# A decoder step on one core: levels 32 and 64 of a triangular inverse as products of 32x32 and 64x64 tiles, and the modulation in column halves

## What is computed

```python
for layer in range(DEPTH):                                  # DEPTH = 2, D = 1024
    mod = (silu(c) @ w_ada[layer] + b_ada[layer])           # c: 9 rows (prompt + 8 sequences), w_ada: 1024 x 6144
    shift1, scale1, gate1, shift2, scale2, gate2 = split(mod, 6)
    h = rms_norm(x, g_norm1[layer]) * (1 + scale1) + shift1
    proj = h @ w_in[layer]
    o_a = gdn_mixer(...)                                    # gated delta rule, 4 heads x 128, below
    o_b = conformer_conv(...)                               # causal depthwise convolution of width 31
    x = x + gate1 * (concat([o_a, o_b]) @ w_out[layer])
    h = rms_norm(x, g_norm2[layer]) * (1 + scale2) + shift2
    f = swiglu(h, ...) if layer == 0 else moe_swiglu(h, ...)  # dense, then top 2 of 8 experts
    x = x + gate2 * f
# inside the gated delta rule, for each head and block of tokens:
a_mat = where(strict, (k * beta) @ k.T * decay, 0.0)
t_inv = triangular_solve(eye + a_mat, eye)                  # inverse of a unit lower triangular matrix
u, w = t_inv @ (v * beta), t_inv @ (k * beta * exp(gc))
```

## Time and profile before

| | |
|---|---|
| median of 3 runs | 1647.95 us (1646.57 to 1649.50) |
| the profiled execution: time | 1647.72 us |
| its span in the trace | 1645.9 us |
| busy in the span | PE 98%, PEld 55%, DVE 47%, ACT 23%, POOL 8% |
| the chain that ended last | PE 90%, DVE 6%, ACT 2%, DMA 1% |
| mean granted clock of PE | 0.979 |

### The profile page before, as it was taken

How to read it: one execution, slowest core, us unless ns; L and a number is a source line. 1 busy time by engine, 2 the same in 40 slices (tenths; PEclk the granted TensorE clock), 3 DMA queues, 4 the chain that set the end, 5 groups by cost and what they waited for, 6 DMA issues and landing times.

```text
span 1645.9 us, 31324 instructions
## 1 busy us (share of the span) xinstructions
PE 1612.4 (98%) x12975; PEld 902.8 (55%) x12975; DVE 773.0 (47%) x1852; ACT 378.3 (23%) x617; POOL 123.5 (8%) x162
## 2 busy tenths in 40 slices
PE   6999999999999999999999999999999999999997
PEld 3878977999998879763333333333333333333333
DVE  2799656454438995462323333334234243243254
ACT  3346524443334454220001010010010100100102
POOL 0122205000012121030000000000000000000100
PEclk9999999999999998978999999999999999999999
DMA  9877029983647760165999999999999999999998
GB/s 383 347 304 257 27 84 370 410 317 128 241 147 301 290 270 1 58 245 194 397 404 407 420 421 410 420 411 420 418 401 420 420 410 420 401 421 420 405 421 372
DMA packets 82375, 535.35 MB, mean 325 GB/s; under 512 B 9184, under 2 KB 9312, under 8 KB 23488
## 3 DMA queue, kind: packets, MB, share of 16 engines
q1 hardware_dynamic: 70592, 487.46, 73.7%
q0 software_dynamic: 10080, 40.47, 6.3%
q10 hardware_dynamic: 1568, 5.51, 0.9%
HBM read 516.24 MB, written 36.04 MB: 336 GB/s over the span
## 4 chain that ended last, share of the span: by engine, by line
PE 90%; DVE 6%; ACT 2%; DMA 1%; issue 1%; SPq 0%; DVEq 0%
PE ps L2448 44%; PE ps L2457 6%; PE ps L1933 6%; PE ps L1934 5%; PE ps L1935 5%; PE ps L2122 4%; PE ps L2293 4%; PE ps L2474 3%; DVE yc L1337 2%; PE ps L1944 1%; PE ps L2030 1%; PE ps L2045 1%; PE ps L2043 1%; PE ps L1984 1%; PE ps L2063 1%; PE ps L2430 1%
## 5 line engine op out<-in xcount | busy, mean ns | idle before, releaser
L2474 PE MATMUL ps<-raw,hT 128*32 128x512 f32 x996 | 432.8, 592 | 0.0
L2474 PE MATMUL ps<-extra,hT 128*32 128x512 f32 x972 | 421.9, 592 | 0.0
L2448 PE MATMUL ps<-extra,ht 128*32 128x512 f32 x2736 | 403.4, 595 | 0.7 <-DVE ht L1843 0.7
L2448 PE MATMUL ps<-raw,ht 128*32 128x512 f32 x2640 | 387.8, 592 | 0.0
L1858 DVE TENSOR_TENSOR ae<-ps,sge 96x512 f32<-96x512 f32 x56 | 38.4, 686 | 514.9 <-PE ps L2448 514.9
L2448 PEld LDWEIGHTS ps<-extra,ht 128*32 128x32 f32 x2736 | 109.2, 110 | 270.4 <-issue 270.3
L2448 PEld LDWEIGHTS ps<-raw,ht 128*32 128x32 f32 x2640 | 104.9, 110 | 256.9 <-issue 256.1
L1819 DVE STREAM_TRANSPOSE hT<-ae 32x128 f32<-32x128 f32 x672 | 202.9, 302 | 17.8
L1210 ACT ACTIVATE sge<-ps 96x512 f32<-96x512 f32 x56 | 33.2, 592 | 705.8 <-PE ps L2448 705.6
L1933 PE MATMUL ps<-h_hi,whi 128*128 128x288 f32 x560 | 168.3, 300 | 0.2 <-DVE h_lo L1321 0.2
L1934 PE MATMUL ps<-h_lo,whi 128*128 128x288 f32 x560 | 166.2, 297 | 0.0
(11 more groups left out here) (367 smaller groups left out, 1804.7 us busy)
## 6 DMA issues: line engine op xcount, KB each, us to landing
raw<-units SPq DMA_DIRECT2D x279, 1024.0 KB, 12.2
extra<-units SPq DMA_DIRECT2D x174, 1024.0 KB, 13.9
slots_in<-const_in POOLq DMA_DIRECT2D x18, 512.0 KB, 30.6
slots_out<-const_in POOLq DMA_DIRECT2D x18, 512.0 KB, 31.6
raw<-units SPq DMA_DIRECT2D x16, 512.0 KB, 7.1
sst<-gdn_in POOLq DMA_DIRECT2D x8, 512.0 KB, 7.3
gdns_out<-sst POOLq DMA_DIRECT2D x8, 512.0 KB, 4.0
qst_out<-qpad POOLq DMA_DIRECT2D x2, 1890.0 KB, 10.7
```

The lines of the kernel that those rows point to most:

```text
L2448: last = mm(ps[rows(t), (G_BANK if kind == "g" else U_BANK) + n % 2, :], ht[n // FC % 2][:, a], weights((kind, n, k // 4), k % 4), start=( ...
L2474: last = mm(ps[GROUPS * GT:P, DOWN_BANK[t][half], :], hidden(n, t, k), weights(("d", n, half), k), start=(c == 0 and first), stop=(n in st ...
```

## The change

Two edits. At levels 32 and 64, `level_pm` and `level_q` multiply only the tiles that are not zero, and `inverse_level` subtracts only these; `tiles_at(s)` gives the ranges of rows and columns of the upper and the lower half of each diagonal square. Levels 2 to 16 and the sample block stay as they are, and so do `level_mask` and `copy_pm` at all levels. In the modulation, a partial sum now takes two of the eight parts more into one accumulation, and the four quarters of the partitions hold two column halves times two partial sums; so the tile is 128 x 256, the copy half as wide, and `ada_columns` has two products with 18 moving columns for four with 9.

```diff
--- before.py
+++ after.py
@@ -245,8 +245,9 @@
 FAR = 30000.0
 LOG_EXP = "natural_log_exp_and_others"
 LEVELS = [2, 4, 8, 16, 32, 64]
+TILED = 32
 CCOL, NCONST = columns(
-    [("ones", P), ("comb", NC_), ("eps6", 1), ("eps5", 1), ("epsq", 1), ("one", 1), ("ident", P), ("tri", P), ("after", P), ("m1l", P), ("m1t", P)]
+    [("ones", P), ("comb", 2 * NC_), ("eps6", 1), ("eps5", 1), ("epsq", 1), ("one", 1), ("ident", P), ("tri", P), ("after", P), ("m1l", P), ("m1t", P)]
     + [(f"mt{s}", P) for s in LEVELS] + [("outA", P), ("outQ", P), ("outAS", TS), ("outQS", TS)]
     + [("pick", 2 * 8), ("before", P), ("iota", P), ("triS", P), ("afterS", P), ("seqp", NB),
        ("ipart", 1), ("valid", 1),
@@ -284,7 +285,7 @@
     put("outQS", np.where(same & (i <= j), FAR, -FAR)[:TS, :TS])
     put("seqp", np.arange(P)[:, None] % TS // TD == np.arange(NB)[None, :])
     put("pick", np.concatenate([np.eye(P // 4)[:, P // 4 - 2 * 8:]] * 4))
-    put("comb", np.concatenate([np.eye(P // 4, NC_)] * 4) * (i % (P // 4) < NC_))
+    put("comb", np.kron(np.kron(np.eye(2), np.ones((2, 1))), np.eye(P // 4, NC_)))
     put("eps6", np.full((P, 1), 1e-6))
     put("eps5", np.full((P, 1), 1e-5))
     put("epsq", np.full((P, 1), P * 1e-6))
@@ -294,6 +295,11 @@
     put("rank", np.broadcast_to(NE - np.tile(np.arange(NE), 3)[None, :], (P, 3 * NE)))
     put("eye8", np.eye(NE))
     return c
+
+
+def tiles_at(s):
+
+    return [(slice(2 * s * j, 2 * s * j + s), slice(2 * s * j + s, 2 * s * (j + 1))) for j in range(P // (2 * s))]
 
 
 class Steps:
@@ -842,7 +848,7 @@
             def row_copy(l, m, place, bank):
                 n = ADA_AT[LANDS["ada", l, 2 * m + 1]]
                 act.wait_ge(ada_used, n + 1)
-                act.activation(modrow[place][n // 2 % len(modrow[place])][:, :], ps[:, bank, :], ACT.Copy).then_inc(row_ready, 1)
+                act.activation(modrow[place][n // 2 % len(modrow[place])][:, 0:2 * P], ps[:, bank, 0:2 * P], ACT.Copy).then_inc(row_ready, 1)
 
             def rsqrt(out, in_, scale, eps, done):
 
@@ -1493,6 +1499,14 @@
                 half = lambda t, i: t.rearrange("p (g c) -> p g c", c=2 * s)[:, :, i * s:(i + 1) * s]
                 L, LT = blk[b]["L"][0:n, 0:H * n], blk[b]["LT"][0:n, 0:H * n]
                 bank, c = Q_AT[blk_i]
+                if s >= TILED:
+                    L3, LT3, Q = heads(blk[b]["L"], n, n), heads(blk[b]["LT"], n, n), bank_heads(Q_AT[blk_i], n, n)
+                    for up, low in tiles_at(s):
+                        if not final:
+                            dve.tensor_tensor(L3[low, :, up], L3[low, :, up], Q[low, :, up], ALU.subtract)
+                        last = dve.tensor_tensor(LT3[up, :, low], LT3[up, :, low], Q[up, :, low], ALU.subtract)
+                    last.then_inc(l_ready, 1)
+                    return
                 if not final:
                     dve.tensor_tensor(half(L, 0), half(L, 0), half(ps[0:n, bank, c:c + H * n], 0), ALU.subtract)
                 dve.tensor_tensor(half(LT, 1), half(LT, 1), half(ps[0:n, bank, c:c + H * n], 1), ALU.subtract).then_inc(l_ready, 1)
@@ -1940,18 +1954,22 @@
                 for half in halves:
                     u = LANDS["ada", l, 2 * m + half]
                     pe.wait_ge(raw_in[u % NRAW], 16 * (u // NRAW + 1))
-                    for k in range(4):
-                        last = mm(ps[32 * k:32 * k + 32, bank, :], cst3[:, 4 * half + k], raw[u % NRAW][:, k * 512:(k + 1) * 512],
-                                  start=(half == 0), stop=(half == 1))
+                    for k in range(0, 4, 2):
+                        for q in range(4):
+                            a, p = divmod(q, 2)
+                            last = mm(ps[32 * q:32 * q + 32, bank, 0:2 * P], cst3[:, 4 * half + k + p],
+                                      raw[u % NRAW][:, (k + p) * 512 + 2 * a * P:(k + p) * 512 + 2 * (a + 1) * P],
+                                      start=(half == 0 and k == 0), stop=(half == 1 and k == 2))
                     last.then_inc(ada_used, 1)
 
             def ada_columns(l, m, place, bank=7):
 
                 n = ADA_AT[LANDS["ada", l, 2 * m + 1]] // 2
                 pe.wait_ge(row_ready, n + 1)
-                for q in range(4):
-                    c = (4 * m + q) * NC_
-                    last = mm(ps[:, bank, c:c + NC_], modrow[place][n % len(modrow[place])][:, q * P:(q + 1) * P], cc("comb"), start=True, stop=True)
+                cols = ps[:, bank, 4 * m * NC_:4 * (m + 1) * NC_].rearrange("p (a i c) -> p a i c", a=2, i=2)
+                for i in range(2):
+                    last = mm(cols[:, :, i], modrow[place][n % len(modrow[place])][:, i * P:(i + 1) * P],
+                              cc("comb").rearrange("p (a c) -> p a c", a=2), start=True, stop=True)
                 last.then_inc(modT_ready, 1)
 
             def ada_run(pairs, banks, place):
@@ -2020,15 +2038,19 @@
                     last = pe.transpose(bank_heads(AT_AT[blk_i], n, n)[:, h], heads(blk[b]["da"], n, n)[:, h], cc("ident", n, n))
                 last.then_inc(at_done, 1)
 
-            def level_pm(l, b, blk_i, n, q):
+            def level_pm(l, b, blk_i, n, q, s):
                 pe.wait_ge(mt_ready, 13 * l + q + 1)
                 if q in (0, 1, 12):
                     pe.wait_ge(low_ready, 3 * l + blk_i + 1)
                 else:
                     pe.wait_ge(l_ready, 13 * l + q - 1)
+                MT, L, PM = heads(blk[b]["MT"], n, n), heads(blk[b]["L"], n, n), bank_heads(PM_AT[blk_i], n, n)
                 for h in range(H):
-                    last = mm(bank_heads(PM_AT[blk_i], n, n)[:, h], heads(blk[b]["MT"], n, n)[:, h], heads(blk[b]["L"], n, n)[:, h],
-                              start=True, stop=True)
+                    if s < TILED:
+                        last = mm(PM[:, h], MT[:, h], L[:, h], start=True, stop=True)
+                        continue
+                    for up, low in tiles_at(s):
+                        last = mm(PM[low, h, up], MT[up, h, low], L[up, h, up], start=True, stop=True)
                 last.then_inc(pm_done, 1)
 
             def level_q(l, b, blk_i, n, q, s, final):
@@ -2038,6 +2060,15 @@
                     pe.wait_ge(linit_ready, 3 * l + blk_i + 1)
                     pe.wait_ge(qk_ready, 3 * l + blk_i + 1)
                 LT, PM = heads(blk[b]["LT"], n, n), heads(blk[b]["PM"], n, n)
+                if s >= TILED:
+                    Q = bank_heads(Q_AT[blk_i], n, n)
+                    for h in range(H):
+                        for up, low in tiles_at(s):
+                            if not final:
+                                mm(Q[low, h, up], LT[low, h, low], PM[low, h, up], start=True, stop=True)
+                            last = mm(Q[up, h, low], PM[low, h, up], LT[low, h, low], start=True, stop=True)
+                    last.then_inc(q_done, 1)
+                    return
                 if not final:
                     for h in range(H):
                         mm(half(bank_heads(Q_AT[blk_i], n, n)[:, h], 0), LT[:, h], half(PM[:, h], 0), start=True, stop=True)
@@ -2135,7 +2166,7 @@
                 cols = [slice(0, P), slice(P, 2 * P), slice(TP, T)]
                 for i in range(len(LEVELS)):
                     for b in range(2):
-                        level_pm(l, b, b, P, 2 * i + b)
+                        level_pm(l, b, b, P, 2 * i + b, LEVELS[i])
                     for b in range(2):
                         level_q(l, b, b, P, 2 * i + b, LEVELS[i], i == len(LEVELS) - 1)
 
@@ -2182,7 +2213,7 @@
                 outputs(l, 0, P)
                 state_rows(l, 0, 7)
                 conf_part(l, 0)
-                level_pm(l, 2, 2, TS, 12)
+                level_pm(l, 2, 2, TS, 12, 2)
                 pe.wait_ge(nw_ready, l + 1)
                 pe.wait_ge(s_ready, 2 * l + 1)
                 new_values(l, 1, P, 4)
```

## The result

The changed kernel takes 1650.68 us, the median of 20 runs (1645.05 to 1655.96), beside 1645.91 for 20 runs of the kernel before (1642.54 to 1651.17). The ratio is 1.0024, with a 95% interval of 1.0013 to 1.0035: 4.0 us slower, and clear of no change. The forecast was 1646.9 us against a median of 1647.95 for before, thus 1 us faster.

A forecast was written before the change was run, and what follows sets the result against it. TensorE was taken to bound the kernel, nine tenths of the span. Level 32 -3.2, norm -0.6, router -0.6, clock +1.4 and +2.2 made -0.8 us from 1647.72: forecast 1646.9 us, range 1642.5 to 1651.5.

The forecast's parts named there:

- the sum's clock term for the blocks: State products (L2063) in both layers' blocks: clock falls earlier, costing 1.1 us a layer, 2.2 in all, bounds 0 to 5.2.
- Level 64: Inverse, level 64: TensorE's work halves but is covered by 2.64 us of VectorE's other work, so counted as nothing.
- Where the clock is low now it can't fall twice: Layer 1's L2063, already part low: argument against the rival in which the clock decides; no size of its own.
- Level 32: Inverse, level 32: 32x32 products at 34 ns, subtractions 0.2 us apart; last correction 1.6 us earlier a layer, 3.2 for two.
- Layer 0's projection: Eight modulation pairs hidden behind VectorE; TensorE waits 2.9 us before the fourth sum of squares, low clock charged 1.4 us.
- Layer 1's projection: Four modulation pairs there, behind VectorE or ScalarE: no gain, and no clock charge.
- Modulation elsewhere: Pairs at layer 1's first norm save 0.6 us and those ahead of the router 0.6; row copy about 370 ns.
- the dense stage's part: One modulation pair in the dense stage: may give 0.4 us, left out of the sum.
- The clock decides: Rival: slack TensorE brings low clock after layer 0's wait and over all L2063; +4.1 us, 1651.8; chance 0.15.

The follow-up runs named there:

- e3: Kernel before with only level 64 of the inverse in tiles, level 32 and modulation as before: 1651.93 us, ratio 1.0040 to the kernel before.
- e4: Kernel before with levels 32 and 64 in tiles and unused TensorE products behind both levels' corrections, modulation as before: 1646.14 us, ratio 0.9997.
- e13: Kernel before with level 64 in tiles, two and four unused products there, and state products at 64 moving columns: 1638.66 us, ratio 0.9963.
- e15: Whole change plus unused products at both levels and layer 0's third sum of squares made four times, thin state products: 1643.35 us, ratio 0.9982 to before.
- e16: Kernel before with level 32 in tiles and unused products there, state products at 8 moving columns, modulation as before: 1646.23 us, ratio 1.0002.
- e14: Kernel before with level 32 tiles and unused products, 64-column state products, modulation in column halves, layer 0's third sum made four times: 1633.24 us, ratio 0.9925.
- e6: Kernel before with state products given 64 moving columns where they had 8: 1638.79 us, ratio 0.9956 to the kernel before.
- e10: Kernel before with level 32 in tiles, two and four unused products there, and state products at 64 moving columns: 1633.20 us, ratio 0.9911.

## Why the prediction was wrong, point by point

**What failed** is the sum's clock term for the blocks, "I charge 1.1 a layer, 2.2, bounds 0 and 5.2". From the tiles alone (6.1 us slower by the ratio) and the 4.1 us that the two inverses gained, it is 10 us for the two layers; the two traces of the table have 8.4 (6.64 and 1.74). Either is beyond the upper bound of 5.2. The mechanism was in the sum, and its size was wrong. The 1.1 also does not follow from the figures ahead of it: with L2063 at the 6.1 us taken there, layer 0 loses 2.6 and layer 1 0.9, 3.5 together. Three things went into the miss.
- The charge ended with L2063. In layer 0's trace the state products lose 3.2 us (3.47 to 6.63) of the 6.64. The low clock lasts through L2112, L2208 and L2128, full-width products without a wait, and the products just ahead of and behind the state products lose 1.9. The last 1.5 come later, where a second low stretch lasts 6.8 us (215.7 to 222.5) for 3.4 before.
- "Level 64. ... I cost that at nothing" was right about the work and wrong about the time. The cover that hid the gain is a queue of VectorE, and behind it TensorE now stood idle where it had worked (in e3 it is busy 40.42 of the 42.00 us of layer 0's blocks, before 41.95): level 64's tiles alone cost 6 us and save none.
- "Where the clock is low now it can't fall twice" holds for L2063 in layer 1 (5.18 to 6.63 us, +1.5), not for the stretch as a whole. Before, the clock fell 2.6 us behind the start of `new_values` and stayed low for 10.2 us; now it falls 3.1 us ahead of it and stays low for 17.1.

**Level 32**: right in its mechanism, 2.0 and 2.1 us a layer where I said 1.6. The terms in it were off both ways. The products are faster than any price I took. From the timeline of the changed kernel, PE in layer 0:

```profile
187.14 0.44 PE L2053 MATMUL ps<-L,MT 32*32 32x32 f32 x16
187.41 0.42 PE L2053 MATMUL ps<-ctmp,MT 32*32 32x32 f32 x16
```

16 start within 0.27 us, 17 ns each, half of my 34. The Trainium skill's TensorEngine Tiling (Array Packing), Restrictions and Gotchas, has it that different row tiles can't access one PSUM bank simultaneously. My reading of it, that the price therefore stays at 34 to 45 ns, isn't borne out: the trace shows a lower price with just such tiles. (At 45 ns the prediction's own steps give 0.8 us a layer, not 0.7.) VectorE's subtractions went the other way. The eight are 0.30 us apart, not 0.20, and follow each other without a gap, so that they and not TensorE set level 32's end. First and last of the eight, from the same timeline:

```profile
188.96 0.28 DVE L1506 TENSOR_TENSOR L<-L,ps 32x128 f32<-32x128 f32 x1 [1.41 <-PE ps L2069]
...
191.05 0.28 DVE L1507 TENSOR_TENSOR LT<-LT,ps 32x128 f32<-32x128 f32 x1
```

**Layer 0's projection**: as forecast. The fourth sum of squares waits 2.98 us, the clock falls behind it, and the mixer starts 1.40 us later (I charged 1.4). The timeline's row, and under it the stretches:

```profile
133.09 1.45 PE L2106 MATMUL ps<-qsq,con 128*128 128x512 f32 x2 [2.98 <-DVE gain L1273]
```

```profile
132.00:134.00 2.00, 0.91 (x2) 0.50 (x3) 1.97 (x7) 1.97 (x3) 0.00 (x0) 0.94 1.08 441
134.00:136.00 2.00, 2.00 (x5) 1.24 (x4) 2.00 (x5) 1.94 (x4) 0.00 (x0) 0.50 1.02 438
136.00:138.00 2.00, 2.00 (x7) 1.43 (x7) 2.00 (x6) 1.97 (x4) 0.00 (x0) 0.71 0.92 391
```

**Layer 1's projection**, "behind VectorE or ScalarE, nothing": the four pairs are indeed hidden (+4.60 before, +4.62 at the sums of squares), but I did not ask there what I had asked in layer 0. A wait of 1.56 us is new, the old one of 2.18 follows, and the low clock behind that is 6.8 us (summed over stretches of 1 us) where the earlier trace rows have 3.4: +1.7, a term that my sum lacked.

**Modulation elsewhere**: 0.66 at norm 2 and 0.66 ahead of the router, where I had 0.6 and 0.6; the dense stage's part, which I left out, is within the -0.52 up to norm 2. The halved tiles are as priced, the copy 373 ns for my 370. Part of the router's gain is lost again in the router (+0.83). In all the modulation is neutral (1.0003), and its own terms, -0.66 - 0.66 + 1.40 + 1.71 with up to -0.52 from the dense stage, make +1.3 us, which lies within the interval.

**The rivals.** "The clock decides", 1651.8 us, had the right mechanism and came out 3.9 us above the median that the forecast started from; measured is 4.0. I gave it 0.15. Its reckoning, though, took L2063 alone and two low stretches in the projection, and the true bill is spread over more products. What spoke for a larger chance was in the rows: a full clock over L2063 in layer 0 and a fallen one in layer 1, thus a place on the edge, and an edit that takes more than half of TensorE's 9.5 us of work ahead of it (an estimate: level 32 ahead of the fall of the clock in the changed kernel, 1.8 us busy, and level 64 in e3, 2.4). The Trainium skill's rule (Perfetto Trace Analysis, Matmul Optimizations), that the matmul engine scales power by utilization and matmuls should run back to back, agrees with the covers of e4 (6.6 us off) and e13 (9.4 by the medians, 7.4 by the ratios); the trace adds that back to back is not enough, since the state products were that already.

**What stays open.** The cover works on waits and on the amount of work at once, so these runs don't say how the two weigh at level 64. Nor do they say why the losses of the two levels don't add. With thin state products, the whole change with cover is 2.7 us faster than before (e15), and level 32's tiles with cover are level with it (e16), though e15 has level 64's tiles and the modulation more; the intervals (0.9966 to 0.9998 and 0.9989 to 1.0015) overlap, and why that order, if it is one, I can't tell from single traces. A version of e14 with level 64's tiles too wasn't tried.

## What to carry to other kernels

Where TensorE is the bound and a stage has thin products, less work for TensorE in front of it can cost more than it saves; work that is hidden behind another engine's queue is worth nothing when taken away, and may be what keeps the clock up. Look at the granted clock of the stretch behind an edit first, and price a low stretch to where it ends, not to the end of the first product group. When products cost the same with more moving columns, widening thin ones, or unused products in the waits, are cheap experiments: here they took 7 us off the kernel before and, with level 32's tiles, 14, where the change as it was had cost 4.

## What the runs showed of the hardware

- A MATMUL with 128 stationary columns takes 0.11 us with 8 or with 64 moving columns (32 in 3.47 us in the kernel before, in 3.52 in e6 and in e10). In the kernel before the granted clock falls behind those with 8; with 64 (e6) it doesn't, TensorE being busy throughout in both (41.95 and 41.93 of 42.00 us).
- Once at 0.50, the clock stayed there through some 14 us of gapless products, full-width ones among them (194.7 to 208.8 us in the changed kernel). It outlasted TensorE's waits, the last of which ended at 194.7.
- 32x32 products on alternating tiles start 17 ns apart, against 34 for 128x32 ones with 32 moving columns on one column group.
- A VectorE subtraction on 32 partitions and 128 columns follows the next at 0.30 us, one on 128 partitions and 256 columns at 0.34; two pieces with an eighth of the elements each (0.60) cost nearly twice the one that they replace.
- The changed kernel's runs differ by 11 us (1645 to 1656), along with their mean clock (0.976 at the fast end, 0.968 to 0.970 at the slow end).
